# A hybrid decoder step: the score products of the two attention maps are issued apart, and ScalarE scales the attention output rows

## The reference, cut to what matters

```python
q, k = ... # (positions, head, map, 64): two maps of 64 columns per head
s = jnp.einsum('bqhmd,bkhmd->bhmqk', q, k2) * (QK_HEAD_DIM ** -0.5)
s = jnp.where(dist >= 0, s + bias, NEG_INF)
p = jax.nn.softmax(s, axis=-1)
a = p[:, :, 0] - lam * p[:, :, 1]
o = jnp.einsum('bhqk,bkhd->bqhd', a, v)
o = rmsnorm(o, subln_gain, SUBLN_EPS) * (1.0 - lam_init)
```

## Time and profile before

| quantity | value |
|---|---|
| median of 3 runs | 1362.29 us (1362.23 to 1364.62) |
| the profiled execution | 1361.42 us |
| its span in the trace | 1359.7 us |
| PE busy in the span | 1318.5 us (97%) |
| DVE, ACT, POOL busy | 723.1, 446.4, 172.7 us |
| granted TensorE clock | 0.999 of full (2.4 GHz) |
| attention loop on PE | 281 to 442 us |

### The profile page before, as it was taken

One profiled execution on the slowest core, in us unless ns is written; L12 is line 12 of the kernel. 1 busy time (PEld: TensorE's weight loads), 2 busy tenths in 40 slices (PEclk: granted clock), 3 DMA queues, 4 the chain that ended last, 5 costly groups with the idle time before them and its releaser, 6 DMA issues.

```text
span 1359.7 us, 21879 instructions
## 1 busy us (share of the span) xinstructions
PE 1318.5 (97%) x8386; PEld 1189.5 (87%) x8386; DVE 723.1 (53%) x1175; ACT 446.4 (33%) x751; POOL 172.7 (13%) x323
## 2 busy tenths in 40 slices
PE   7999999978879999999999999999999999999998
PEld 6999999955546788998999989898989898989986
DVE  6447633166677664565354454546463645453555
ACT  6321012045566633352232313131323132322332
POOL 2227000022223221200000000000000000000003
PEclk9999999999999999999999999999999999999999
DMA  8676875278794632222010202020111101020117
GB/s 270 194 255 233 271 240 162 73 201 214 185 262 123 209 124 86 79 77 78 16 62 22 71 15 77 15 77 15 62 31 62 31 28 64 15 77 15 47 47 136
DMA packets 115672, 146.97 MB, mean 108 GB/s; under 512 B 8012, under 2 KB 83445, under 8 KB 115605
## 3 DMA queue, kind: packets, MB, share of 16 engines
q1 hardware_dynamic: 107865, 122.30, 30.1%
q10 hardware_dynamic: 6748, 20.24, 4.0%
q0 software_dynamic: 992, 3.54, 1.6%
HBM read 114.06 MB, written 31.47 MB: 107 GB/s over the span
## 4 chain that ended last, share of the span: by engine, by line
PE 90%; DVE 3%; issue 3%; POOL 2%; ACT 1%; DMA 1%; SPq 0%; DVEq 0%; POOLq 0%; ACTq 0%
PE PS L2410 39%; PE PS L2132 17%; PE PS L2475 16%; PE PS L2353 7%; PE PS L2225 2%; PE PS L2490 2%; PE PS L2505 2%; POOL small L1408 1%; PE PS L2285 1%; PE PS L2187 1%; DVE PS L1577 1%; PE PS L2117 1%; PE PS L2344 1%; DMA x_in<-in_x_prompt_dram 1%; PE PS L2213 0%
## 5 line engine op out<-in xcount | busy, mean ns | idle before, releaser
L2410 PE MATMUL PS<-act_lo,wu_hi 128*128 128x364 f32 (+1 forms) x1056 | 346.4, 328 | 0.0
L2410 PE MATMUL PS<-act_hi,wu_lo 128*128 128x364 f32 (+1 forms) x1056 | 346.0, 328 | 0.0
L2410 PE MATMUL PS<-act_hi,wu_hi 128*128 128x364 f32 (+1 forms) x1056 | 345.9, 328 | 0.0
L2410 PEld LDWEIGHTS PS<-act_hi,wu_hi 128*128 128x128 f32 x1056 | 198.5, 188 | 0.5
L2410 PEld LDWEIGHTS PS<-act_lo,wu_hi 128*128 128x128 f32 x1056 | 198.2, 188 | 0.4
L2410 PEld LDWEIGHTS PS<-act_hi,wu_lo 128*128 128x128 f32 x1056 | 198.3, 188 | 0.0
L1892 DVE TENSOR_TENSOR y_acc<-y_acc,PS 128x512 f32<-128x512 f32 x162 | 111.2, 687 | 115.9 <-PE PS L2475 115.9
L2475 PE MATMUL PS<-wd_hi,g_hi 128*128 128x512 f32 x324 | 130.1, 402 | 0.0
L2475 PE MATMUL PS<-wd_lo,g_hi 128*128 128x512 f32 x324 | 128.0, 395 | 0.0
L2475 PE MATMUL PS<-wd_hi,g_lo 128*128 128x512 f32 x288 | 114.0, 396 | 0.0
L1278 ACT CAST g_hi<-conv 128x1088 fp32r<-128x1088 f32 x21 | 23.2, 1105 | 245.6 <-PE PS L2475 189.6
(11 more groups left out here) (289 smaller groups left out, 2324.2 us busy)
## 6 DMA issues: line engine op xcount, KB each, us to landing
wu_raw<-in_w_up_dram SPq DMA_DIRECT2D x44, 512.0 KB, 4.0
k_tok<-in_cache_k_dram SPq DMA_DIRECT2D x64, 256.0 KB, 4.0
keys_t<-k_turned ACTq DMA_DIRECT2D x32, 512.0 KB, 4.2
vpage<-in_cache_v_dram SPq DMA_DIRECT2D x64, 256.0 KB, 4.2
wd_raw<-in_w_down_dram SPq DMA_DIRECT2D x22, 512.0 KB, 5.3
w_raw<-in_w_in_dram SPq DMA_DIRECT2D x20, 512.0 KB, 6.4
kt_mid<-keys_t SPq DMA_DIRECT2D x20, 256.0 KB, 6.2
kt_b<-keys_t SPq DMA_DIRECT2D x20, 256.0 KB, 6.5
```

The costliest lines, as they stand in the source:

```text
L2410: mm = nc.tensor.matmul(PS[:, 3 * half + c, 0:kept(c)], a[:, half, k, :], b[:, k, KEPT[c]], start=(j == 0), stop=(j == len(parts) - 1))
```

## The change

Four edits, all in the attention loop:

1. `scores` loops over the maps outside and over the parts inside, and takes a list of maps. For 20 of the steps (`first_map_ahead`: 3, 5 to 7, 10, 13 to 15, 18, 21 to 31) the product of map 0 is issued in the iteration before, ahead of `turn(i - 1)`, and the product of map 1 at its old place. Each product now waits for `prob_ready` of its own map alone.
2. `smp_scores(i)` goes to the front of the iteration, except where `i % 4 == 0`.
3. DVE's `near_max(i, 0)` (and `far_max(i, 0)`) go ahead of `mix(i - 1)`.
4. `out_norm` moves from DVE to ACT (the last three stay on DVE), without the gain; ACT's `out_square` goes between the two exponents. The gain is applied by `take_out`, where it is one number per partition (`gain_col`). The tile `sub_gain`, its transfer and its scaling go.

```diff
@@ SyncE, setup
-                sp.dma_start(sub_gain[:], subln_gain[0:1, :].to_broadcast([P, DV])).then_inc(setup_loaded, 16)
@@ ScalarE
+        def out_norm(i):
+            act.wait_ge(ofac_ready, i + 1)
+            if i >= QB:
+                act.wait_ge(ot_ready, (i - QB) // OB + 1)
+            nc.scalar.activation(o_nrm[:, i % QB, :], PS[:, out_bank(i), 0:DV], ACT.Copy,
+                                 scale=o_fac[:, i % 4:i % 4 + 1]).then_inc(onrm_ready, 1)
+
         def take_out(g):
...
-            nc.scalar.copy(res[:, g * OB // QB, c0:c0 + P * OB], PS[:, bank, :]).then_inc(ot_taken, 1)
+            nc.scalar.activation(res[:, g * OB // QB, c0:c0 + P * OB], PS[:, bank, :], ACT.Copy, scale=gain_col).then_inc(ot_taken, 1)
...
         for i in range(NSTEP):
-            if i >= 3:
-                out_square(i - 3)
             if i >= 1 and late_exponent(i - 1) and i % 8 == 4:
                 smp_exponent((i - 1) // 8, 0)
+            if i >= 3:
+                out_norm(i - 3)
             if i >= 2:
                 take_turned(i - 2)
...
                 exponent(i, 0)
+                if 2 <= i < NSTEP - 1:
+                    out_square(i - 2)
...
                 exponent(i, 1)
@@ VectorE
         for i in range(NSTEP):
-            if i >= 2 and early(i):
+            if i >= 2:
                 if wide_step(i):
                     far_max(i, 0)
-                    far_max(i, 1)
+                    if early(i):
+                        far_max(i, 1)
+                    near_max(i, 0)
                 else:
-                    near_max(i, 0)
-            if i == 3:
-                out_norm(i - 3)
+                    if i - 1 not in JOINED:
+                        near_max(i, 0)
             if i >= 1:
                 mix(i - 1)
...
-            for m in range(2):
+            if i >= 2:
                 if wide_step(i) and not early(i):
-                    far_max(i, m)
-                if i >= 3 and m == 0 and wide_step(i) and not i == 3:
-                    out_norm(i - 3)
-                if i >= 2 and (wide_step(i) or not early(i) or m == 1):
-                    near_max(i, m)
-                if i >= 3 and m == 0 and not wide_step(i) and not i == 3:
-                    out_norm(i - 3)
+                    far_max(i, 1)
+                if i - 1 in JOINED:
+                    near_max(i, 0)
+                near_max(i, 1)
@@ TensorE
-        def scores(i, only=None):
+        def scores(i, only=None, maps=(0, 1)):
...
-            for j, (c, e) in enumerate(parts):
-                if only is not None and j != only:
-                    continue
-                user = bank_user(i, 1 if second_bank(i) else j)
-                if user >= 0:
-                    pe.wait_ge(prob_ready, 2 * user + 2)
-                for m in range(2):
-                    d = slice(DH * m, DH * m + DH)
+            for m in maps:
+                d = slice(DH * m, DH * m + DH)
+                for j, (c, e) in enumerate(parts):
+                    if only is not None and j != only:
+                        continue
+                    user = bank_user(i, 1 if second_bank(i) else j)
+                    if user >= 0:
+                        pe.wait_ge(prob_ready, 2 * user + m + 1)
                     mm = nc.tensor.matmul(score_cols(i, m)[:, c:e], qT[d, h, qs], kT[d, h, NS + c:NS + e], start=True, stop=True)
...
         for i in range(NSTEP):
+            if samples_first(i):
+                smp_scores(i)
             if i in PARTED:
                 scores(i, 1)
+            elif first_map_ahead(i) and i >= 3:
+                scores(i, maps=(1,))
             elif i >= 2 and i - 1 not in JOINED:
                 scores(i)
...
                 if i + 1 in PARTED:
                     scores(i + 1, 0)
+                elif i >= 2 and first_map_ahead(i + 1):
+                    scores(i + 1, maps=(0,))
                 if i >= 1:
                     turn(i - 1)
```

More of the change, by code:

```diff
@@ L145, in _program @@
     gain = keep.put("gain", [P, D])
-    sub_gain = keep.put("sub_gain", [P, DV])
+    keep.put("spare2", [P, DV])
     small = keep.put("small", [P, 256])
@@ L801, in load_pair @@
                 sp.dma_start(k_tok[b][:, a, :], cache_k[0, bass.ds(page, 1)].rearrange("a t h d -> t (a h d)")).then_inc(slot_loaded[b % 3], 16)
-        sp.wait_ge(setup_loaded, 16 * 6)
+        sp.wait_ge(setup_loaded, 16 * 5)
         for p in range(4, 2 * len(GROUPS)):
@@ L958, in take_job @@
                 act.wait_ge(line_stored, 16)
-                act.wait_ge(lam_step, 3)
+                act.wait_ge(lam_step, 2)
                 w = KEPT[c].stop - KEPT[c].start
@@ L1059, in out_square @@
                                  scale=precip[:, i % 4, 0:1], accum_out=o_ssq[:, i % 4:i % 4 + 1]).then_inc(osq_ready, 1)
+        def out_norm(i):
[4 more added lines that the diff above has]
+                                 scale=o_fac[:, i % 4:i % 4 + 1]).then_inc(onrm_ready, 1)
         def take_out(g):
+            if g == 0:
+                act.wait_ge(rowcoef_step, 2)
             act.wait_ge(ot_ready, g + 1)
@@ L1490, in lam_tables @@
         def lam_tables():
-            dve.wait_ge(setup_loaded, 16 * 6)
+            dve.wait_ge(setup_loaded, 16 * 5)
             nc.vector.tensor_tensor(lam_prod[:], lam_in[:, 0:2, :], lam_in[:, 2:4, :], ALU.mult).then_inc(lam_step, 1)
-            nc.vector.tensor_scalar(sub_gain[:], sub_gain[:], 1.0 - LAM_INIT, None, ALU.mult).then_inc(lam_step, 1)
-            dve.wait_ge(lam_step, 2)
+            dve.wait_ge(lam_step, 1)
             dve.wait_ge(const_ready, 4)
@@ L1598, in out_norm @@
                 dve.wait_ge(ot_ready, (i - QB) // OB + 1)
-            nc.vector.scalar_tensor_tensor(o_nrm[:, i % QB, :], PS[:, out_bank(i), 0:DV], o_fac[:, i % 4:i % 4 + 1], sub_gain[:],
-                                           ALU.mult, ALU.mult).then_inc(onrm_ready, 1)
+            nc.vector.tensor_scalar(o_nrm[:, i % QB, :], PS[:, out_bank(i), 0:DV], o_fac[:, i % 4:i % 4 + 1], None,
+                                    ALU.mult).then_inc(onrm_ready, 1)
         def place_queries():
@@ L1695, in ahead @@
             nc.vector.tensor_scalar(lam_dif, lam_exp[:, 1:2], LAM_INIT, None, ALU.subtract).then_inc(lam_step, 1)
-            dve.wait_ge(lam_step, 4)
+            dve.wait_ge(lam_step, 3)
             nc.vector.tensor_tensor(neg_lam, lam_dif, lam_exp[:, 0:1], ALU.subtract).then_inc(lam_ready, 1)
@@ L2291, in smp_weigh, with samples_first, first_map_ahead @@
             mm.then_inc(pv_ready, 1)
+        def samples_first(i):
+            return i >= 2 and i % 4 != 0
+        def first_map_ahead(i):
+            return 2 <= i < NSTEP and i not in PARTED + JOINED and i - 1 not in JOINED and i not in (QB + 3, 2 * QB + 3)
         for i in range(NSTEP):
+            if samples_first(i):
+                smp_scores(i)
             if i in PARTED:
                 scores(i, 1)
+            elif first_map_ahead(i) and i >= 3:
+                scores(i, maps=(1,))
             elif i >= 2 and i - 1 not in JOINED:
@@ L2312, in _ @@
                 smp_scores(0)
-            if i >= 1:
+            if i >= 1 and not samples_first(i):
                 smp_scores(i)
```

## The result

| | median us (range, runs) | profiled run | span |
|---|---|---|---|
| before | 1362.97 (1362.23 to 1364.62, 4) | 1361.42 | 1359.7 |
| after | 1375.98 (1374.16 to 1376.61, 4) | 1376.61 | 1374.9 |

The ratio is 1.0092, with a 95% interval of 1.008 to 1.0104: slower by 13.0 us. The forecast was 1371.2, which is 8.9 above the median that it started from (1362.29). Direction and range held, the size was too small.

A forecast was written before the change was run, and what follows sets the result against it. PE was taken to bound the kernel, with 26.8 us idle in the attention loop against 27 us added. Stretch terms 5.0 + 1.4 + 1.0 + 2.7 - 1.2 = +8.9 on 1361.4 gave 1370.3, plus 0.9 for the median: 1371.2 us, range 1362.5 to 1377.

The forecast's parts named there:

- The mechanism: Score products: the two maps of a part run together; one issued alone pays full price, 1.71 us at width 7.
- Both waits of the earlier trace: PE waits in the loop: scores for exponents (11.3 us), `weigh` for the scaled row (10.8); both to fall below 3.
- over 93%: Sign in the next profile: PE's busy share of the attention loop, with busy time up by 20 us or more.
- likeliest case: Whole kernel: the forecast itself, slower at 1371.2 us, own range 1366 to 1375, chance 0.63.
- a new chain on top: Rival: square, POOL, scaling, copy and `weigh`, in order on ACT, lengthen 16 wide steps; +14, 1376 us, chance 0.15.
- the first term: Two score calls for one in 20 steps: 27 us more PE time, as much as all the loop's idle time.
- Iteration 14: A wide step after the change: 6.1 us of PE work against 5.67 before, both waits gone, PE the bound.
- The third -0.4: Iterations 11 and 12 and their like: idle 2.6 us, added 1.5; -0.4 taken three times, -1.2 in all.
- Stalls at 16 to 18: ACT's row scaling ahead of `take_turned` and the sample exponent waits for POOL: stalls grow by some 0.5 us.
- Head 3: Iteration 23 to output projection: about 53 us for 47.9; idle 4.5 all filled, 9.2 added, +5.0 with 0.3 delay.
- `take_out`: The copy with a scale costs what the plain copy did: zero, at worst 8 x 0.1 us.
- The transfer on SP: Dropping `sub_gain`, 0.43 us of SP's queue: zero, since the next issue is held by a wait.

The follow-up runs named there:

- x6_apart: Kernel before with only PE's list changed: in the same 20 steps the sample scores stand between the two maps' products; 1372.01 us, ratio 1.0064.
- x1_pairs: Changed kernel with both maps of a part issued together again at the old place and DVE's maxima in the old order; 1366.04 us, ratio 1.0028.
- x4_loops: Kernel before with only the loops of `scores` exchanged, maps outside and parts inside, waits and places as before; 1363.51 us, ratio 0.9999.
- x12_square: Changed kernel with the square sum of steps 9, 17 and 28 moved behind ACT's two sample copies; 1374.41 us, ratio 1.007.
- x2_norm_only: Kernel before with edit 4's row scaling on ACT and gain in `take_out`, the square staying at the start of the step; 1365.27 us, ratio 1.0016.
- x5_cross: Changed kernel, but in 14 steps map 1 of step i and map 0 of step i+1 follow each other; 1374.77 us, ratio 1.0077.
- x8_head3: Changed kernel with no score call ahead in steps 24 to 31, keeping separate waits and maps outside; 1375.82 us, ratio 1.0093.
- x3_split_only: Changed kernel with the row scaling back on DVE, behind `mix`; 1413.58 us, ratio 1.0332.

## Why the prediction was right in direction and too small

- **The mechanism held.** Two maps of one step run in the array together, and issued alone each pays the full time: 1.70 us measured for a forecast 1.71. Both waits of the earlier trace rows fell below 3 us, and PE's own queue became the bound: 95% of the loop (166.29 of 175.67), where "over 93%" was forecast. x6_apart shows that the split alone costs 8 us, and x1_pairs that taking it back returns 10.
- **The number is that of a rival, its mechanism is not.** 1376.0 us lies in the stated range, but just outside the likeliest case's own (1366 to 1375) and on the 1376 of "a new chain on top". That rival doesn't hold: PE waits by name for 9 us in all, not for more than 12, and x1_pairs, which keeps the whole chain on ACT, came back to 1366.
- **The step that failed is the first term: "Added PE time: 109 x 0.21 + 20 x 0.2 = 27 us".** The loop's busy time grew by 166.3 - 134.2 = 32.1. The other side of the sum, how much idle time is filled, was nearly right: 17.4 us filled (26.8 - 9.4), and 27 - 8.9 = 18.1 in the forecast. So it is PE's price, and not the order, that was short by 5.
- **Two sources of that 5 us.** Both are sized in the two profiled runs. The first is what stands behind a lone call. Iteration 14 was forecast at 6.1 and took 6.29: `weigh` takes 1.31 (350.27 to 351.58) for 1.19 before, and `turn` 0.80 (353.49 to 354.29) for the 0.7 I had put. Each lone call brings one more change from 64-row to 128-row products and back; 20 steps x 0.19 = 3.8 us is an estimate from this one iteration. Single records bear the cause out. In x1_pairs the second record of a `weigh` starts 0.21 us behind the first where a score call stands ahead (348.99), and 0.11 where `turn_out` does (355.14). In the changed kernel the score product behind `weigh` starts 0.21 us after its last record (351.37), where `turn` in x1_pairs needs 0.11. It isn't the rows alone: from `turn` to the sample scores, both of 128 rows but of 128 and 32 columns, it is 0.20 too.
- **The second source is TensorE's clock.** At 363 us PE had been busy 0.81 of 2 us; then:

```profile
361.00:363.00 2.00, 0.81 (x10) 0.44 (x12) 1.44 (x5) 2.00 (x7) 0.00 (x0) 1.00 0.07 19
363.00:365.00 2.00, 2.00 (x14) 1.34 (x9) 1.82 (x11) 0.24 (x2) 0.00 (x0) 0.53 0.00 0
365.00:367.00 2.00, 2.00 (x13) 2.00 (x13) 0.47 (x3) 0.12 (x1) 0.00 (x0) 0.62 0.05 12
```

  `weigh` with 14 records took 3.0 us there (363.68 to 366.68), and the same call in the first head 1.67 (317.80 to 319.47). Some 1.3 us are lost. The forecast had no term for the clock, as the trace before showed 1.00 in the stretches of the earlier trace rows. But this loss doesn't belong to the change. x4_loops, as fast as the kernel before, has it at the same place, 3.12 us (363.93 to 367.05) for the 1.63 of the trace before:

```profile
363.93 3.33 PE L2225 MATMUL PS<-v_all,at_sb 128*128 128x128 f32 x14 [0.32 <-DVE o_nrm L1599]
```

  The profiled run before (1361.42 us, granted clock 0.999) lies below all four runs of its median, and the run of the changed kernel with the same 0.999 took 1374.16 us, 12.7 more. So the clock explains part of the gap between the two traces, and little of the 13.0 us between the medians.
- **By stretch** (forecast, measured, each against the profiled run before; the stretches are those of the sum):

| iterations | forecast | measured |
|---|---|---|
| to 4 | 0 | -0.3 |
| 5 to 7, 13 to 15 | +0.7, +0.7 | +0.8, +0.7 |
| 8 to 10, 16 to 18 | +1.35, +1.35 | +2.1, +3.7 |
| 11 and 12, 19 and 20 | -0.4, -0.4 | -0.2, -0.2 |
| 21 and 22 | +1.0 | +1.0 |
| 23 to 31 | +5.0 | +7.1 |

  The third -0.4 of the forecast fell on steps before 5, where -0.3 came. For 13 to 15 the forecast's own terms give 3.6 - (3.4 - 0.73) = 0.9 and not the 0.7 that I put, so that the 0.7 was met is luck. The rows make 14.7 with the rounding; 0.6 more came behind the loop, 15.2 in span. The medians lie 13.0 apart, since this profiled run is the slowest of four.
- **Stalls at 16 to 18.** I had put 0.5 for ACT's row scaling. It costs 0.37 as forecast, but the moved square was the cost that I had left out there: in step 9 ACT does it first and copies `s_own` last, and PE waits (x12_square, 1.6 us for three steps):

```profile
325.28 0.34 ACT L1057 ACTIVATE PS<-PS,small 128x128 f32<-128x128 f32 x1 [2.09 <-PE PS L2232]
325.64 0.46 ACT L1041 ACTIVATE prob<-PS,small 128x256 f32<-128x256 f32 x1
326.09 0.58 ACT L1101 COPY s_at<-PS 128x512 f32<-128x512 f32 x1
326.55 0.21 ACT L1103 COPY s_own<-PS 64x64 f32<-64x64 f32 x1
```

  At 16 to 18 the loss of clock above comes on top.
- **Head 3.** "About 53" was 55.0. Busy time rose by 9.4 (52.80 - 43.41), the 9.2 of the forecast. But 2.2 us of idle time stayed where I had "everything is filled": the out projection waits 0.98 for the last `take_out`, a score call 0.53, and the rest are waits of 0.2 to 0.25. Nor is the lone call the whole price here. x1_pairs, with the pairs back, still loses 4.1 us against the kernel before from `weigh(25)` to the output projection, where the changed kernel loses 4.5; in the steps ahead, `weigh(21)` to `weigh(25)`, it takes 22.7 us for 27.4. So in the last steps edits 2 and 4 open waits of their own (the two rows of x1_pairs above), which the lone calls here for the most part fill; the forecast had no term for them.
- **`take_out`** with a scale takes 687 ns for 587 of the copy: 0.1 each, my "at worst". The transfer on SP was worth nothing, as forecast.
- **What a forecast of the edits one by one would have shown.** Edits 2 and 4 together cost little (x1_pairs +2.4, and edit 4 alone +1.6 in x2_norm_only): a small gain in the wide steps, and the loss behind `weigh(25)`. The new chain on top didn't decide: ACT waits 47.4 us for `weigh` ahead of the square and PE waits for ACT nowhere for long.

## What to carry to other kernels

When two products share the array, their pair is one unit: filling a wait by pulling one of them forward buys the wait at the price of the whole call. Before moving a product into a gap, count its length as if it ran alone, and weigh the sum of those lengths, with the changes of shape behind them, against all idle time; here 32 us of work went into 27 us of gaps. A partner from another step serves as well (x5_cross), but the second starts only when its own wait is met (x8_head3), so both waits must be met at about the same time.

## What the runs showed of the hardware

- Two score products in different halves of the rows run together when another product of the first half stands between them in the program (x4_loops, 1.71 us) and when they belong to different steps (x5_cross, 1.93 us for a width 7 and a width 8 call).
- The second of two such products starts when its own wait is met, while the first is running: 0.05 us after the exponent in x8_head3 (409.78 to 409.83).
- A change of shape from one product to the next costs about 0.1 us: 0.21 us from record to record for 0.11 (x1_pairs, 348.99 against 355.14).
- The granted clock fell to 0.50 for 45 us inside busy attention work in x3_split_only and to 0.53 to 0.62 for 4 us in the changed kernel, each time behind a stretch in which PE was busy for 65% (2.61 of 4 us) or 40% (0.81 of 2) of the time. A fall at the same place stands in x4_loops, whose time is that of the kernel before. Not every such stretch was followed by a fall, and what decides stays open.
- POOL's small tensor-tensor operation on 128x1 took 549 ns on the mean in the changed kernel for 868 before (minimum, median, maximum below; after, then before). It goes with the place of the square, which starts POOL's work, and not with DVE's order or the row scaling: x1_pairs, with the square between the exponents and DVE's old order, has 549 too, and x2_norm_only, with the square at the start of the step and no row scaling on DVE, 874. That it was long because DVE was at work beside it is a guess. What it gained isn't shown; in the changed kernel PE waits for nothing of this chain for long.

```profile
L1418 POOL TENSOR_TENSOR small<-small x32: 548/548/562, 288.7 to 468.2; 128x1 f32<-128x1 f32 x32
```
```profile
L1408 POOL TENSOR_TENSOR small<-small x32: 548/551/1587, 289.5 to 453.8; 128x1 f32<-128x1 f32 x32
```
